# Down projection as Strassen blocks over a ring of hidden pairs, and a query-head norm folded into the softmax

## The reference, cut to what matters

```python
aq = rope(rms_norm_2(aq.reshape(B, S, ATTN_HEADS, HEAD_DIM), q_norm_w[l]), pos)
s = jnp.einsum('bnqkgd,bnjkd->bnkgqj', qb, kb).astype(jnp.float32) * scale
m = jnp.maximum(jnp.max(s, axis=-1, keepdims=True), sink_l)
p = jnp.exp(s - m)
p = p / (jnp.sum(p, axis=-1, keepdims=True) + jnp.exp(sink_l - m))
...
h = h + jnp.concatenate([y_attn, y_ret], axis=-1) @ w_out[l]
m = rms_norm_2(h, ffn_norm_w[l])
h = h + (jax.nn.silu(m @ w_gate[l]) * (m @ w_up[l])) @ w_down[l]
```

## Time and profile before

| what | value |
|---|---|
| median of 3 runs | 2276.56 us (2275.07 to 2280.46) |
| the profiled execution | 2281.95 us |
| its span, first to last instruction | 2280.2 us |
| instructions | 31148 |
| mean granted clock of TensorE | 0.993 |
| PE busy | 2253.9 us, 12508 matmuls |
| VectorE (DVE) busy | 1387.1 us |
| ScalarE (ACT) busy | 784.1 us |
| GpSimd (POOL) busy | 525.6 us |
| DMA | 208.56 MB, mean 91 GB/s |

### The profile page before, as it was taken

One profiled execution on the slowest core, in us unless ns is written; L12 is line 12 of the kernel. 1 busy time (PEld: TensorE's weight loads), 2 busy tenths in 40 slices (PEclk: granted clock), 3 DMA queues, 4 the chain that ended last, 5 costly groups with the idle time before them and its releaser, 6 DMA issues.

```text
span 2280.2 us, 31148 instructions
## 1 busy us (share of the span) xinstructions
PE 2253.9 (99%) x12508; PEld 1875.6 (82%) x12508; DVE 1387.1 (61%) x2283; ACT 784.1 (34%) x1309; POOL 525.6 (23%) x386
## 2 busy tenths in 40 slices
PE   8999999999999999999999999999999999999999
PEld 7888888887888888888888888878878888888887
DVE  4667787678857444664367787744866666631323
ACT  5323423333334333233234445422333333342210
POOL 3312222122213221242122132100122222250300
PEclk9999999999999999999999999999999999999999
DMA  4121121222233335743122121143222222162242
GB/s 153 48 58 51 50 63 39 61 63 60 69 102 112 114 110 211 269 139 132 58 75 57 42 52 42 39 134 111 84 83 84 84 84 83 65 211 73 81 141 72
DMA packets 245951, 208.56 MB, mean 91 GB/s; under 512 B 44080, under 2 KB 217776, under 8 KB 245808
## 3 DMA queue, kind: packets, MB, share of 16 engines
q1 hardware_dynamic: 245808, 206.57, 29.1%
HBM read 152.00 MB, written 47.71 MB: 88 GB/s over the span
## 4 chain that ended last, share of the span: by engine, by line
PE 88%; DVE 6%; DMA 1%; POOL 1%; issue 1%; ACT 1%; SPq 1%; DVEq 0%; ACTq 0%
PE PS L120 85%; PE PS L123 3%; SPq L146 1%; DMA HloF<-in_w_out_dram 0%; DVE Wlo L129 0%; POOL sm L129 0%; DVE Nn L129 0%; DVE T3f L129 0%; DMA Wraw<-in_w_in_dram 0%; DVE Ntmp L129 0%; ACT junk L126 0%; DVE Yt L137 0%; DVE sm L1993 0%; DMA ro<-qr 0%; DMA rot<-ro 0%
## 5 line engine op out<-in xcount | busy, mean ns | idle before, releaser
L120 PE MATMUL PS<-Hhi,Whi 128*128 128x512 f32 (+1 forms) x1544 | 497.3, 390 | 2.4 <-DVE Hlo L129 2.1
L120 PE MATMUL PS<-Hhi,Wlo 128*128 128x512 f32 (+1 forms) x1544 | 499.0, 392 | 0.0
L120 PE MATMUL PS<-Hlo,Whi 128*128 128x512 f32 (+1 forms) x1544 | 498.3, 391 | 0.0
L120 PEld LDWEIGHTS PS<-Hhi,Whi 128*128 128x128 f32 x1544 | 287.5, 190 | 58.8 <-issue 4.7
L120 PEld LDWEIGHTS PS<-Hhi,Wlo 128*128 128x128 f32 x1544 | 286.6, 190 | 57.8 <-issue 5.3
L120 PEld LDWEIGHTS PS<-Hlo,Whi 128*128 128x128 f32 x1544 | 285.5, 190 | 55.5 <-issue 3.3
L126 ACT ACTIVATE Whi<-Wraw 128x512 fp32r<-128x512 f32 x218 | 135.3, 622 | 526.9 <-PE PS L120 523.3
L129 POOL TENSOR_TENSOR Wlo<-Wraw,Whi 128x512 fp32r<-128x512 f32 x82 | 120.1, 1466 | 430.5 <-ACT Whi L126 430.4
L129 DVE TENSOR_TENSOR Wlo<-Wraw,Whi 128x512 fp32r<-128x512 f32 (+1 forms) x136 | 113.0, 834 | 161.7 <-ACT Whi L126 161.0
L129 DVE TENSOR_TENSOR Ntmp<-Nn 32x30 f32<-32x30 f32 (+14 forms) x240 | 91.6, 382 | 28.2 <-DMA Nn<-scr_ns 23.3
L120 PE MATMUL PS<-YMhi,Whi 128*128 128x512 f32 (+1 forms) x300 | 99.2, 378 | 0.0
(11 more groups left out here) (421 smaller groups left out, 4373.1 us busy)
## 6 DMA issues: line engine op xcount, KB each, us to landing
Wraw<-in_w_in_dram SPq DMA_DIRECT2D x126, 256.0 KB, 2.9
scr_g<-stg SPq DMA_DIRECT2D x24, 512.0 KB, 3.0
tg<-scr_g SPq DMA_DIRECT2D x24, 512.0 KB, 4.6
scr_fb<-fb SPq DMA_DIRECT2D x22, 512.0 KB, 4.1
fin<-scr_fb SPq DMA_DIRECT2D x22, 512.0 KB, 4.1
gwA<-in_w_in_dram SPq DMA_DIRECT2D x40, 256.0 KB, 3.4
wA<-in_w_gate_dram SPq DMA_DIRECT2D x38, 256.0 KB, 3.2
wA<-in_w_up_dram SPq DMA_DIRECT2D x38, 256.0 KB, 3.3
```

The lines of the kernel that those rows point to most:

```text
L120: return self.h.matmul(out, lhsT, rhs, start=start, stop=stop, skip_group_check=True)
```

## The change

It does the following:

- The down projection becomes 16 Strassen blocks (kind "w") in four rounds of four; the block `b` makes two output tiles (`dp = b % 4`). The 22 hidden tiles are 11 pairs, and a round covers some of them (`WINDOWS`).
- The pairs lie in a ring of four slots. Per pair 4 quarters of 256 KB are loaded, VectorE makes T1 to T4 and their lo (8 instructions of 512 columns), ScalarE makes 7 hi, and GpSimd 3 lo (B11, B22, B21).
- The results of each block are added up in SBUF: by ScalarE (5) and VectorE (3) in the first round, then by VectorE alone (8 a block, 11 in the last round). The weights are loaded per block as A11, A21, A22 and A12, with VectorE's 7, ScalarE's 7 and GpSimd's 4 instructions, 256 or 384 columns wide.
- The query tiles are no longer multiplied by 1/rms. The tile is copied out of PSUM with the norm's weight as scale, after the Square; 1/rms is given to the Exp of the softmax as its scale, the maximum is multiplied by it, and the sink column is multiplied by rms. The 8 broadcast transposes, the broadcast copy and the 2 multiplications fall away per query tile.
- The rows of `w_out_2` come in one DMA per 128 rows instead of two for the first four.
- The values of two attention blocks are put together on PE, and `ORDER` and `PICKS` are new for every engine and every stage.

The diff, cut to its core:

```diff
-GROUPS = [list(range(0, 8)), list(range(8, 15)), list(range(15, 22))]
+WINDOWS = [(0, 1)] + 3 * [(0, 1, 2)] + [(2, 3, 4)] + 3 * [(3, 4, 5)] + [(5, 6, 7)] + 3 * [(6, 7, 8)] + [(8, 9, 10)] + 3 * [(9, 10)]
...
+PRODUCTS["w"] = (("A11", "B11", "a"), ("S3", "T3", "d"), ("S4", "B22", "e"), ("S2", "T2", "b"), ("S1", "T1", "c"),
+                 ("A12", "B21", "a"), ("A22", "T4", "d"))
...
+    def slot_read(self, block, i):
+        if i > 3:
+            return ("prod", TAKEN_BY[block], ("w", LAST_TAKEN[i - 4]))
+        return ("prod", "A22", LAST["f"]) if i < 2 else ("tile", ("fu", 21))
...
+    def down_products(b):
+        P, bank = K.bp["w"], {}
...
+            for k, i in enumerate(pairs):
+                bhi, blo = K.ring[block, i % 4]
+                pe.wait_ge(*S.fbh_act.at((block, i)))
+                pe.mm(bank[out], hi[:, k, :], bhi[:], first and k == 0, False)
+                pe.wait_ge(*K.hidden_lo(block, i))
+                pe.mm(bank[out], hi[:, k, :], blo[:], False, False)
+                pe.wait_ge(*K.sum_lo(name, b))
+                t = pe.mm(bank[out], lo[:, k, :], bhi[:], False, i == pairs[-1])
...
@@ PE, key_stream @@
-            for hf in range(2):
+            for hf in range(0 if kind == "aq" else 2):
...
@@ ScalarE, key_stream and attention @@
+            elif kind == "aq":
+                act.wait_ge(*S.dense_pe.at(("tile", me)))
+                src = banks.of(("dp", me))
...
+                act.act(raw[:], src, ACT.Copy, scale=K.qn8).then_inc(*S.key_act.tick(("raw",) + me))
...
+                        scale=K.q_rstd[j % 2][:, 2 * b + h:2 * b + h + 1], accum_out=su[:, h:h + 1]).then_inc(*at_act.tick(("e", n)))
...
@@ VectorE, attention and feed_forward @@
-            dve.ts(nm, mx, -1.0, ALU.mult).then_inc(*at_dve.tick(("nm", n)))
+            dve.stt(mr, mx, -1.0, K.q_rstd[j % 2][:, 2 * b:2 * b + 2], ALU.mult, ALU.mult).then_inc(*at_dve.tick())
+            dve.stt(nm, sk, -1.0, mr, ALU.mult, ALU.min).then_inc(*at_dve.tick(("nm", n)))
...
+            yield from add(x6, "a", b, "A11", "x1")
+            yield from add(c22, "d", b, "S3", "u2")
+            yield from add(c12, "e", b, "S4", "g2")
+            yield from add(x6, "b", b, "S2", "x6")
+            if g == len(WINDOWS) // 4 - 1:
+                for c in (c12, c22, c21):
+                    dve.tt(c[:], c[:], x6[:], ALU.add).then_inc(*S.ffn_dve.tick())
+            yield from add(c12, "c", b, "S1", "cb")
+            yield from add(c22, "c", b, "S1", "cc")
+            yield from add(c11, "a", b, "A12", "ca")
+            yield from add(c21, "d", b, "A22", "cd")
...
@@ VectorE, hidden @@
+            for step in ("T1", "T3", "T2", "lo T3", "lo T2", "lo T1", "T4", "lo T4"):
...
@@ GpSimd, key_stream and hidden @@
+                pool.tt(K.q_rstd[p % 2], K.st2, K.expo[:, 0:16], ALU.pow).then_inc(*S.key_pool.tick())
+                pool.tt(K.q_rms[p % 2], K.st2, K.q_rstd[p % 2], ALU.mult).then_inc(*S.key_pool.tick(("st", me)))
...
+            for block, last in (("B11", "T1"), ("B22", "T2"), ("B21", "T4")):
+                pool.tt(lo[:], K.raw[block, i % 4][:], hi[:].bitcast(F32), ALU.subtract).then_inc(*S.ffn_pool.tick(("lo", block, i)))
...
@@ SyncE, out_weights_2 @@
-            if k < 4:
-                for a, h in enumerate((k, k + 4)):
-                    sp.dma(K.HloF[64 * a:64 * a + 64, k, :], w_out2[h * 64:h * 64 + 64, :]).then_inc(*sig[k % 4].tick(k, by=16))
-            else:
-                sp.dma(K.HloF[:, k, :], w_out2[k * 128:(k + 1) * 128, :]).then_inc(*sig[k % 4].tick(k, by=16))
+            sp.dma(K.HloF[:, k, :], w_out2[k * 128:(k + 1) * 128, :]).then_inc(*sig[k % 4].tick(k, by=16))
```

More of the change, by code:

```diff
@@ L753, in gemms @@
             yield from dense([tile], K.YMhi, K.YMlo, m_ready, dps=three)
[L754 to L760, removed]
+        for b in BLOCKS_W:
+            yield from down_products(b)
     SINGLE = tuple(f"B{i}" for i in range(8))
@@ L767, in block_products @@
                 "c": S.ffn_dve.at(("v", b)), "d": S.ffn_dve.at(("u1", b)), "e": S.ffn_dve.at(("g2", b))}
-        for name, block, out in P.first if b in OPEN.values() else P.products:
+        for name, block, out in P.first if b in (OPEN["g"], OPEN["f"]) else P.products:
             first = out not in bank
@@ L789, in block_products @@
                 if k == 3:
+                    t.then_inc(*S.dense_pe.tick(("prod", name, b)))
+                yield
+    def down_products(b):
+        P, bank = K.bp["w"], {}
+        own = S.ffn_act if b[1] < 4 else S.ffn_dve
+        read = {"a": [own.at(("ca", b))], "b": [S.ffn_dve.at(("x6", b))], "c": [S.ffn_dve.at(("cc", b))],
+                "d": [own.at(("cd", b))], "e": [own.at(("g2", b))]}
+        for name, block, out in P.products:
+            first = out not in bank
+            if first:
+                bank[out], before = banks.take(("st", out, b), SINGLE, read[out])
+                for m in before:
+                    pe.wait_ge(*m)
+            elif out == "a":
+                pe.wait_ge(*own.at(("x1", b)))
+            else:
+                pe.wait_ge(*own.at(("u2", b)))
+            pe.wait_ge(*S.sum_act.at((name, b)))
+            hi, lo = P.slots[name]
+            pairs = WINDOWS[b[1]]
+            for k, i in enumerate(pairs):
[6 more added lines that the diff above has]
+                t = pe.mm(bank[out], lo[:, k, :], bhi[:], False, i == pairs[-1])
+                if i == pairs[-1]:
                     t.then_inc(*S.dense_pe.tick(("prod", name, b)))
@@ L2818, in block_weights @@
                 sp.wait_ge(*K.sum_lo("A11", (kind, b[1] - 1)))
-            if kind == "f":
+            if kind == "w":
+                pairs = WINDOWS[b[1]]
+                rows = D["w_down_2"][0][256 * pairs[0]:256 * pairs[-1] + 256, :]
+                w = [(rows, (2 * (b[1] % 4) + m) * 128) for m in range(2)]
+            elif kind == "f":
                 w = [(D[n][0], b[1] * 128) for n in ("w_gate_2", "w_up_2")]
@@ L3070, in lay_out @@
         A[n] = I[n]
+    pairs = [I["w_out_2"][:, 64 * h:64 * h + 64] for p in range(4) for h in (p, p + 4)]
+    A["w_out_2"] = np.concatenate(pairs + [I["w_out_2"][:, 512:]], axis=1)
     return A
```

420 lines of the change are left out of this document (265 added, 155 removed).

## The result

| what | before | after |
|---|---|---|
| median of 7 runs each | 2275.93 us (2273.85 to 2280.46) | 2265.56 us (2260.0 to 2271.97) |
| ratio of the times, 95% interval | | 0.9949 [0.9938, 0.996] |
| profiled execution, and its span | 2281.95, 2280.2 us | 2262.68, 2260.9 us |

What follows compares the result with a forecast made beforehand. PE was taken as the bound (99% busy, 0.2274 us a matmul), less what DVE can't deliver in time. Terms -30.0 + 6.5 + 3 + 1 + 2 - 3.2 - 1.5 - 3 = -25.2 us gave 2251 us, range 2236 to 2268.

Steps and rivals of the forecast that it cites:

- New orders: First layer and attention rearranged with the same work: -3 us (-10 to +8).
- Rival D: Whole kernel: the new orders cost what the projection gains, ending around 2275 us; chance 0.06.
- the forecast's own test: Sign that the forecast is wrong: a first layer longer or shorter by more than 8 us.
- Matmuls: Down projection: 924 matmuls instead of 1056, 132 fewer at 0.2274 us each, -30.0 us.
- DVE in the middle and last blocks and the ring: Down projection: VectorE late in eight middle blocks +6.5 us, in the last four +3, pair loading +1.
- The price per GpSimd operation: Down projection's middle blocks: VectorE loses 0.42 us per GpSimd operation, making a block 15.1 us, 0.8 over PE.
- The ring's step: Pair slots in the down projection: tightest at T3 of pair 4, 5.5 us of slack; +1 us (0 to +5).
- The end: Kernel's end: last output addition starts some 3.2 us after the last matmul instead of 1.5; +2 us (+1 to +3).
- Query norm and output weights: Attention: 32 fewer transposes, -3.2 us; 8 DMAs instead of 12 shorten PE's 3.5 us wait, -1.5 us.
- Both places where a page was weighed: VectorE beside GpSimd: 0.42 us lost, not a whole-operation lock; operations start 0.60 us apart, not after a full drain.

Runs made afterwards that it cites:

- e9: Changed kernel, PE's large products spread evenly between the recurrence's steps in the first layer, four more moved into each unit; 2285.86 us, ratio 1.0031.
- e1: Changed kernel with all engines doing the first layer in the order of the kernel before; 2249.72 us, ratio 0.9875.
- e14: e1 run once more with no edit, beside later runs; 2251.38 us, ratio 0.9885.
- e3: Kernel before with only the new down projection; first layer, attention, query norm and output weights' loads as before; 2259.42 us, ratio 0.9919.
- e12: e1 with GpSimd's 97 lo parts and VectorE's 44 lo of T1 to T4 in the down projection replaced by memsets to zero; 2245.87 us, ratio 0.986.
- e8: e1 with the rows of `w_out_2` loaded in 12 DMAs as before instead of 8; 2252.53 us, ratio 0.988.
- e6: e1 with GpSimd's 97 lo subtractions in the down projection replaced by memsets to zero; 2249.69 us, ratio 0.9868.
- e0: Changed kernel run again with no edit, for a second profile; 2267.02 us, ratio 0.9948.
- e15: Changed kernel, PE's large products laid evenly between the recurrence's steps in the first layer, same number of them; 2274.53 us, ratio 0.9983.

## Why the prediction was wrong

The step that failed is **New orders, -3 (-10 to +8)**. It took the first layer and the attention together, with the argument that PE idles 7 us in the first 240 us and that no row tells a better order from a worse one. Measured apart, the new order of the first layer costs 14 us at the second cut and 15 to 17 by medians, past the upper bound of +8; the attention, with the norm and the output weights in it, gains 10. The bound was drawn too narrow: idle time of 13 us before (of 720) says about how much an order can still win, and nothing of how much another can lose. In a stretch where each unit alternates between a serial recurrence and cover laid by hand, a loss has no such limit, as e9 showed. Rival D, new orders that cost what the projection gains, had the right mechanism and some six tenths of the size (14 to 17 of some 25 us), at a chance of 0.06. And the forecast's own test, a first layer longer or shorter by more than 8 us, is the one that came up. Without this step the sum is 22.2 us. e1 and e14, which have all but the first layer's order, are 26 to 28 us below the kernel before: by medians the down projection gave 18.5 where 17.5 were forecast, and the attention 9.7 where 4.7 were. So the rest came out somewhat better than forecast, and that e1 lies at the 2251 us that were forecast for the whole is chance. What in the new order costs the 14 us is open.

The other steps, each against its term:

- *Matmuls*, -30.0: 132 went, and the feed-forward and down part fell by 20.8 us in the two profiles and by 18.5 in e3's median; 9 to 12 us were given back, where the forecast had 12.5 (6.5, 3, 1 and 2).
- *DVE in the middle and last blocks and the ring*, +10.5: 9 to 12 less 2.8 for the end leaves 6 to 9. e12 takes 4.5 of it away (599.5 in e1 to 595.0). The price per GpSimd operation was right (0.39 for 0.42 us), but its use as a pace was not: with DVE at 90% (152.79 of 169 us, forecast over 75%) PE waits only once a round, at a T3, and between these DVE is in time. GpSimd's own operations were longer than the forecast had them (1.32 and 1.24 us for 384 columns, not 1.0). The ring's step looked for the tight place at pair 4: its lo of T3 was indeed done only 16.5 us into block 3 and not 12.2, with 1 us of slack instead of 5.5, but PE didn't wait there; it waited for pairs 2, 5 and 8, which the forecast hadn't named. PE's matmul waits were 6 us in total, forecast 8 to 15.
- *The end*, +2: the last matmul starts at 2252.66 and the span ends 8.2 us later, before 5.4: +2.8. The end of the changed kernel, timeline:

```profile
2252.32 2.48 DVE L129 TENSOR_TENSOR acc<-PS,acc 128x512 f32<-128x512 f32 x4
...
2252.66 0.39 PE L120 MATMUL PS<-hT4hi,wLoA 128*128 128x512 f32 x1
...
2253.16 2.36 PE L123 MATMUL PS<-cst,acc 128*128 128x128 f32 x16
...
2254.73 2.47 DVE L129 TENSOR_TENSOR ot<-PS,ot 128x512 f32<-128x512 f32 x4
```

  Four sums, 16 transposes and four additions follow one another as the forecast had it; the end of before stands in the earlier trace rows.
- *Query norm and output weights*, -3.2 and -1.5: the attention fell by 9.7 us by medians. The transposes went (rot x72 of the earlier trace rows is now x40), and so did the wait of the earlier trace rows; the longest wait of PE's matmuls that is left, 1140 to 1540 us:

```profile
PE PS L120 <- DVE smx L140: 0.6, 1, 0.6
```

  Before there were 3.5 and 2.3 us. 3.2 us of transposes and 5.2 us of waits make 8.4 of the 9.7. e8 shows that the wait of the earlier trace rows didn't go by the eight loads, so the mechanism of the -1.5 was wrong. What share of the waits' end is the norm's and what the new order's was not tried apart.

Both places where a page was weighed came out for the rows. The Trainium skill ("SBUF — State Buffer", Who interferes with whom) calls the shared ports an exclusive lock, and says that it is held for the whole instruction where it speaks of VectorE's two-port modes. The lengths of e6 agree that VectorE's operations with two SBUF inputs are long only beside GpSimd's reads. The mean loss of 0.39 us, beside GpSimd operations that are 1.25 us long on the mean, would fit meetings in part; how long each meeting was, was not counted. By "VectorE: DVE Perf Modes" (The DRAIN you can't avoid) in the Trainium skill, taken as the prediction took it, the four sums at the end would take four whole lengths, 2.7 us. They take 2.48, which is three starts 0.60 us apart and one length. The same section also says that an operation which is not held starts earlier, which the prediction left out and which the rows bear out.

## What to carry to other kernels

An order written out by hand is a change of its own: cut the span at pieces of work that both kernels have, and run the new order of a stage that the idea doesn't need apart from the idea. Here more than half of what the projection and the attention gained (15 to 17 of 28 us) was lost in the first layer, ahead of them, and undoing it gave the best version. A small idle share says about what a new order can win, not what it can lose; and two causes of lateness on one engine need not add up: here either relief alone let it catch up.

## What the runs showed of the hardware that was not expected

- VectorE's operations lost some 38 us beside 97 operations of GpSimd, and taking that away made the stage 4 to 6 us shorter: an engine that is busy 90% of a stretch can still be in time for PE in nearly every block.
- A memset on GpSimd (0.42 us for 384 columns, 0.53 for 512) beside the same VectorE work cost it nothing (683 ns). A memset writes SBUF and doesn't read it, so the hold comes with GpSimd's reads (groups by form on POOL in e6, 1995 to 2250 us):

```profile
L143 POOL MEMSET wLoA<- 128x384 f32 x36 | 15.1, 419 | 32.4 <-ACT wHiA L126 32.4
```

- Two executions of one kernel differ by 4 us in a single stage that has the same work (the down part in e0 against the first profile, the attention in e14 against e1), and the down part spreads over 5 us in its twelve profiles. A stage's size from one profile is no better than that. In the attention the traces show where most of it lies: three profiles of the new attention (e6, e8, e14) are 526.0 to 527.3 us long and have one wait of PE for the tile `inn` of 2.6 to 2.8 us; the twelve others, 521.2 to 523.3 us, have none above 0.2. In e14 the chain runs there through a load of the rotation (`rot<-ro`, 3.9 us, 1292 us). Why it is late in some executions isn't shown.

**Open.** Which steps of the new first-layer order cost the second 6.6 us was not isolated, nor what in the first 337 us costs the 6.8; the orders of the engines depend on one another, and PE's alone was varied only in e9 and e15. Nor is the attention's gain of 10 us divided between the norm, the new order and the smaller changes there.
